# A one-core decoder step: all rotations on VectorE, fewer small VectorE steps, the normaliser in four strips

## The reference, cut to what matters

```python
xn = rms_norm(x, norm_w)
aq, ak, av, az, mq, mk, mv, mo, mz, ga, gm, mi, mf = split(xn @ w_in)
aq = partial_rope(rms_norm(aq, q_norm_w), pos)     # per head of 128
ak = partial_rope(rms_norm(ak, k_norm_w), pos)
# partial_rope: of 128 channels the first 32 are rotated, halves of 16
out = concat([x1 * cos - x2 * sin, x2 * cos + x1 * sin, rest])
attn = softmax(q k / sqrt(128)) v                  # prompt causal; samples over cached pages
# the samples take, of 4 blocks of 256 cached keys, the 3 with the best mean score
# matrix memory (mLSTM), state C, n, m:
h = num / maximum(abs(den), exp(-m_t))
den = w_inter * (q . n_prev) + sum(s)
n_new = a_prev * n_prev + sum_s a_s k_s
C_new = a_prev * C_prev + sum_s a_s k_s v_s^T
y = x + (sigmoid(ga) * (attn * silu(az)) @ Wa + sigmoid(gm) * (h * silu(mz)) @ Wm) @ w_out
```

## Time and profile before

| | us |
|---|---|
| median of three runs | 473.07 (472.76 to 473.12) |
| profiled execution | 472.86 |
| its span, first to last instruction | 470.7 |

### The profile page before, as it was taken

One profiled execution on the slowest core, in us unless ns is written; L12 is line 12 of the kernel. 1 busy time (PEld: TensorE's weight loads), 2 busy tenths in 40 slices (PEclk: granted clock), 3 DMA queues, 4 the chain that ended last, 5 costly groups with the idle time before them and its releaser, 6 DMA issues.

```text
span 470.7 us, 11313 instructions
## 1 busy us (share of the span) xinstructions
PE 458.8 (97%) x3823; PEld 417.4 (89%) x3823; DVE 402.6 (86%) x1646; ACT 289.5 (61%) x486; POOL 99.8 (21%) x181
## 2 busy tenths in 40 slices
PE   7999999999989999989999999999999999999997
PEld 5899899898779898878899889899899898899997
DVE  4898899699999997999999999889999874667861
ACT  4866545676973685995485695657848357324430
POOL 2040421013323322422321342312223110000000
PEclk9999999999999999999999999999999999999999
DMA  8899599659999999999999999998999995457511
GB/s 302 321 360 406 179 369 325 226 168 350 297 415 407 411 347 335 394 398 411 408 368 313 404 415 408 410 359 304 378 415 408 410 348 192 141 174 270 179 50 46
DMA packets 44993, 150.89 MB, mean 321 GB/s; under 512 B 6332, under 2 KB 7932, under 8 KB 44808
## 3 DMA queue, kind: packets, MB, share of 16 engines
q1 hardware_dynamic: 20368, 70.77, 41.3%
q0 software_dynamic: 19008, 67.20, 37.2%
q10 hardware_dynamic: 5560, 12.21, 6.7%
HBM read 137.37 MB, written 12.76 MB: 319 GB/s over the span
## 4 chain that ended last, share of the span: by engine, by line
PE 69%; DVE 15%; ACT 8%; issue 4%; DMA 3%; ACTq 0%; POOLq 0%; POOL 0%; DVEq 0%
PE pj L535 26%; PE pj L538 13%; PE wk L535 6%; DVE kpages L1169 4%; PE pa L716 4%; DVE wlo L1070 4%; PE wk L538 3%; DMA kpages<-in_cache_k 3%; DVE cslot L1253 2%; ACT L837 2%; ACT whi L817 2%; PE wk L488 2%; PE wk L640 2%; PE wk L672 1%; PE wk L493 1%
## 5 line engine op out<-in xcount | busy, mean ns | idle before, releaser
L535 PE MATMUL pj<-xn,whi 128*128 128x264 f32 x1328 | 180.6, 288 | 0.8 <-ACT mqT L975 0.7
L535 PEld LDWEIGHTS pj<-xn,whi 128*128 128x128 f32 x1328 | 168.4, 189 | 8.8 <-issue 6.6
L1070 DVE TENSOR_TENSOR wlo<-wraw,whi 128x1024 fp32r<-128x1024 f32 x112 | 137.1, 1228 | 8.7 <-ACT whi L817 8.2
L817 ACT ACTIVATE whi<-wraw 128x1024 fp32r<-128x1024 f32 x112 | 117.9, 1053 | 23.2 <-PE wk L538 13.0
L1169 DVE CUSTOM_DVE_ANT_0 kpages<-kpages,qbc 128x128 f32<-128x128 f32 x512 | 114.9, 288 | 1.7 <-DMA kpages<-in_cache_k 1.6
L538 PE MATMUL pj<-xn,wlo 128*128 128x264 f32 x664 | 94.3, 284 | 3.4 <-DVE wlo L1070 3.4
L538 PEld LDWEIGHTS pj<-xn,wlo 128*128 128x128 f32 x664 | 85.5, 188 | 4.5 <-DVE wlo L1070 4.5
L405 POOL DMA_DIRECT2D kpages<-in_cache_k x64 | 34.3, 536 | 175.2 <-DVE sco L1169 152.2
L405 POOL DMA_DIRECT2D vpages<-in_cache_v x64 | 33.9, 530 | 59.1 <-issue 40.1
L1169 DVE DVE_READ_ACCUMULATOR2_ANT sco<- 128x1 f32 x512 | 41.2, 80 | 0.0
L716 PE MATMUL pa<-vpages,prob 128*32 128x256 f32 x512 | 34.3, 385 | 0.7 <-ACT prob L875 0.7
(11 more groups left out here) (277 smaller groups left out, 634.7 us busy)
## 6 DMA issues: line engine op xcount, KB each, us to landing
wraw<-in_weights SPq DMA_DIRECT2D x112, 512.0 KB, 6.7
kpages<-in_cache_k POOLq DMA_DIRECT2D x64, 512.0 KB, 8.3
vpages<-in_cache_v POOLq DMA_DIRECT2D x64, 512.0 KB, 10.9
cslot<-in_states SPq DMA_DIRECT2D x16, 512.0 KB, 8.6
out_C_s<-cslot ACTq DMA_DIRECT2D x16, 512.0 KB, 8.0
xres<-in_tokens SPq DMA_DIRECT2D x1, 1056.0 KB, 6.8
out_k_p<-kT ACTq DMA_DIRECT2D x4, 256.0 KB, 9.8
out_v_p<-v_nat ACTq DMA_DIRECT2D x4, 256.0 KB, 5.0
```

The source lines that it names most:

```text
L535: mm(bank[:, 0:T], whi[:, q, k, :], src[:, g, k, :], start=(k == 0 and g == 0), stop=False)
L817: A(whi[:, n % WSPLIT], wraw[:, n % WRAW], ACT.Copy).then_inc(whi_ready, 1)
L1070: V.tensor_tensor(wlo[:, n % WRAW], wraw[:, n % WRAW], whi[:, n % WSPLIT], ALU.subtract).then_inc(wlo_ready, 1)
```

## The change

- The 32 rotated channels of a head are reordered in the weights, so that the two halves of 16 start 32 partitions apart (`ORDER`: 16 rotated, 16 others, 16 rotated, the rest). Then VectorE can make the rotation by itself: it multiplies partitions 32 to 63 by sin and writes to 0 to 31, and the other way round, and the signs are in the sine table. The product with `rot` is gone on TensorE, for queries and keys, and with it the waits for its bank; `rope_norm` has five instructions, four of which work on 32 or 64 partitions.
- The query rows are made by a product with the permutation `back` instead of by a transpose.
- The eight instructions on the rows of the gates all stand ahead of head 0.
- The new normaliser is made in four strips of 32 partitions: weights are a column of `wt` repeated 32 times, 64 columns of `mk_nat` move, eight products instead of four; the output's layout follows.
- On VectorE: `nm` comes out of the reductions (scale -SCALE, minimum), the `gmax` copy is gone, the two mask additions are one, the samples' denominator is made from already weighted products (order at step 6 changed, two instructions fewer at step 9).

```diff
-            def norm_sums(ss, ro, i, src):
-                mm(ss[:, 0:T], ones, sq[:, i, :], start=True, stop=True)
-                mm(ro[:, 0:T], rot, src, start=True, stop=True).then_inc(norm_ps, 1)
+            def norm_sums(ss, i):
+                mm(ss[:, 0:T], ones, sq[:, i, :], start=True, stop=True).then_inc(norm_ps, 1)
...
                     if g >= 2:
-                        pe.wait_ge(q_ready, g - 1)
+                        pe.wait_ge(rs_ready, g - 1)
...
-                    last = tr(bank[0:NB, (h - first) * P:(h - first + 1) * P], qT[:, h, SEQ:T], P)
+                    last = mm(bank[0:NB, (h - first) * P:(h - first + 1) * P], qT[:, h, SEQ:T], back, start=True, stop=True)
...
-                    for d in range(EC):
-                        for t in range(2):
-                            col = SEQ - 1 if t == 0 else 383
-                            last = mm(wk[3][:, MHD + d:MHD + d + 1], mk_nat[:, t, d * P:(d + 1) * P], wt[:, col:col + 1],
-                                      start=(t == 0), stop=(t == 1))
+                    part = MHD // VG
+                    for t in range(2):
+                        col = SEQ - 1 if t == 0 else 383
+                        for q in range(VG):
+                            last = mm(wk[3][q * VC:(q + 1) * VC, MHD:MHD + part], wt[:, col:col + 1].broadcast_to([P, VC]),
+                                      mk_nat[:, t, q * part:(q + 1) * part], start=(t == 0), stop=(t == 1))
...
+            def rope_norm(x, r, done):
+                low, high, both = slice(0, LO), slice(LO, 2 * LO), slice(0, 2 * LO)
+                ch.step(V.tensor_tensor(hT[low, 0, :], x[high], sin[high], ALU.mult))
+                ch.step(V.tensor_tensor(hT[high, 0, :], x[low], sin[low], ALU.mult))
+                ch.link(V.tensor_tensor(hT[both, 1, :], x[both], cos[both], ALU.mult))
+                ch.link(V.tensor_tensor(x[both], hT[both, 0, :], hT[both, 1, :], ALU.add))
                 V.tensor_tensor(x, x, r, ALU.mult).then_inc(done, 1)
...
-                if h == 1:
+                if h == 0:
                     dve.wait_ge(gate_ln, 1)
...
-                if h == 2:
...
-                if h == 3:
...
-                    ch.step(V.tensor_copy(gmax[:, b, :], gm[:, b % 2, :]))
                     V.tensor_tensor(probs[:, b % 2], sco[:, b % 2],
-                                    gm[:, b % 2, :].unsqueeze(1).broadcast_to([P, PAGES, HEADS]), ALU.subtract).then_inc(pm_ready, 1)
+                                    gmax[:, b, :].unsqueeze(1).broadcast_to([P, PAGES, HEADS]), ALU.subtract).then_inc(pm_ready, 1)
...
-                    V.tensor_scalar(nm[:, n, :], nm[:, n, :], -SCALE, None, ALU.mult).then_inc(smax_ready, 1)
+                    V.tensor_tensor_reduce(att[:, n, 0:P], wk[n][:, 0:P], mask3[:, 0:P], -SCALE, 3.0e38, ALU.add, ALU.min, nm[:, n, 0:1])
+                    V.tensor_tensor_reduce(att[:, n, P:384], wk[n][:, P:384], mask3[:, P:384], -SCALE, 3.0e38, ALU.add, ALU.min,
+                                           nm[:, n, 1:2]).then_inc(smax_ready, 1)
...
-                    ch.step(V.tensor_tensor(wt[:, 0:P], wt[:, 0:P], triT, ALU.add))
-                    V.tensor_tensor(wt[:, SEQ:384], wt[:, P:SEQ], triT, ALU.add).then_inc(wl_ready, 1)
+                    V.tensor_tensor(blocks, wt[:, 0:SEQ].rearrange("p (i t) -> p i t", i=2), triT.unsqueeze(1).broadcast_to([P, 2, P]),
+                                    ALU.add).then_inc(wl_ready, 1)
...
-                    ch.step(V.tensor_tensor(sst[:, 0], qk, w_new, ALU.mult))
-                    V.tensor_tensor(sst[:, 1], qn, w_old, ALU.mult).then_inc(qc_read, 1)
+                    ch.step(V.tensor_copy(sst[:, 0], qk))
+                    ch.link(V.tensor_tensor(sst[:, 2], qn, m_exp, ALU.max))
+                    V.scalar_tensor_tensor(out=sst[:, 2], in0=qn, scalar=-1.0, in1=sst[:, 2], op0=ALU.mult, op1=ALU.max).then_inc(qc_read, 1)
                     dve.wait_ge(qc_read, j + 1)
-                    ch.link(V.tensor_tensor(sst[:, 1], sst[:, 1], sst[:, 0], ALU.add))
-                    ch.link(V.tensor_tensor(sst[:, 2], sst[:, 1], m_exp, ALU.max))
-                    ch.link(V.scalar_tensor_tensor(out=sst[:, 2], in0=sst[:, 1], scalar=-1.0, in1=sst[:, 2], op0=ALU.mult, op1=ALU.max))
```

## The result

The changed kernel takes 478.12 us (median of 4 runs, 477.62 to 480.47) against 473.1 for the kernel before: a ratio of 1.0115 with a 95% interval of 1.0091 to 1.0138. It is slower by 5.0 us by the medians and 5.4 us by the ratio, outside the range of the prediction, on the side to which I gave 24%. The profiled execution took 477.62 us, with a span of 475.5 and a mean granted clock of 0.993.

What follows compares the result with a forecast made beforehand. TensorE and VectorE take turns as the bound. Terms +0.4 - 0.88 + 0.1 + 0.2 + 0.1 + 0.2 + 0.1 - 0.13 - 0.4 sum to -0.3 us: execution 472.5, median 472.8; range 470.0 to 475.1.

Steps and rivals of the forecast that it cites:

- TensorE's head period: Heads, before 50 us: removing the rotation saves TensorE 0.44 us a head, 3.1 us over seven; project 8 ends at 45.0.
- VectorE's rotation: Heads: five steps instead of four, 2.09 us instead of 1.74, +0.35 a rotation (bounds 0 to +0.46), +2.8 over eight heads.
- Rival D: VectorE suffers more: slower products from SBUF, or rotation chained at 0.46 throughout, +0.2 a rotation in 16: 474.4 us; 12%.
- Gates' rows: Moved ahead of head 0 into VectorE's 1.9 us idle time; transfer moves under 1 us, 5 us of slack, no cost or gain.
- Query rows: Behind the wait for the last head: eight products with `back` replace transposes, +0.88 us; step 1's project starts +0.4 later.
- Rival A: The late clock: the wait at 45 to 48 us drops TensorE to the lower level, +2.3 us, 475.1 in all; 16%.
- Round 0: Up to 93.6 us, TensorE leads: two key rotations removed, -0.88 us, and the normaliser's strips +0.1.
- 93.6 to 137: VectorE leads: one longer rotation, +0.35 us, less a `gmax` copy and a mask start-up of about 0.08 each: +0.2.
- 181 to 212: Taken as a copy of the VectorE-led stretch from 93.6 to 137.4 us: +0.2 us.
- 137 to 181 and 212 to 254: Later stretches of the rounds, TensorE leading from 137: +0.1 us each.
- Round 3: Close handover at `wlo`: VectorE +0.2 later against 0.33 spare, so only about 0.13 of TensorE's 0.88 us is gained: -0.13.
- From 306.7: VectorE leads: two instructions of the samples' normaliser removed, one replaced by a copy (0.26 us), and two `gmax` copies (0.15): -0.4.

Runs made afterwards that it cites:

- e4_forms: Changed kernel with the two sine products of query heads 1 to 5 replaced by forms on other partitions, rotation not computed there; ran once, 476.76 us.
- e3_rotation: Kernel before with all rotations on VectorE and query rows by products with `back`, gates' rows left where they were; 481.84 us, ratio 1.0195.
- e13: Changed kernel with the query rows' group behind chunk 9 instead of 8 and five products without use ahead of it; 477.73 us, ratio 1.009.
- e14: Changed kernel with query rows' group behind chunk 9, five products without use ahead, and gates' rows sent ahead of the seven V pages; 475.9 us, ratio 1.0052.
- e1_warm: Changed kernel with nine products without use on TensorE ahead of its wait for the last head; 477.3 us, ratio 1.0096.
- e6b_queries_te: Changed kernel with query rotations back on TensorE, keys on VectorE, the rotation's matrix with 128 columns; 476.08 us, ratio 1.0053.
- e7_behind: Changed kernel with the query rows' group behind chunk 9 instead of chunk 8; 475.66 us, ratio 1.0051.
- e6_queries_te: Changed kernel with query rotations back on TensorE, keys on VectorE, the rotation's matrix with 64 columns; 477.74 us, ratio 1.0105.

## Why the prediction was wrong, step by step

- *What bounds the kernel.* Right: TensorE leads in the head stage and VectorE from 93.6 on. "Work added on VectorE costs only where VectorE leads" was applied with the old leaders. The change itself makes VectorE the leader of the head stage, as my own sum said, and I didn't price what follows from a wait of that length.
- *TensorE's head period* 3.81 to 3.37: step 0 begins 3.1 us earlier. Right.
- *VectorE's rotation.* The first failed step: 0.35 us for the fifth instruction, taken from the spacing of an unchained one. The rotation got 0.55 us longer, and it starts 0.11 later behind a split, 0.66 in all, by three changes of blocks (e4_forms). That is 0.20 more than I had in each of eight heads and 0.11 in the six with a split in front, 2.3 us; the last head came at 50.20 instead of 48.1, 2.1 later. My upper bound, +0.46, didn't take this in, because I bounded the added instruction and not its neighbours. Rival D had the direction and the spacing (0.46 throughout, though by changes of blocks and not by waits) and, with 0.2 a rotation, two thirds of the size.
- *Gates' rows.* Right that they fill VectorE's idle time: without it 1.7 us more (e3_rotation). Right that their transfer is issued hardly earlier (34.3 instead of 35.0). That it lands later, at 50.7 instead of 48.4, and becomes the next bound once the clock is mended, I had not seen (e13, e14). The 5 us of slack were too many: in e13 it lands 6.0 us later than before and step 9 is 2.86 late, so some 3 us were to spare.
- *Query rows* +0.88: right (2.11 against 1.23 us at the full clock).
- *The clock.* The second failed step: the sum has nothing for it. Rival A, at 16%, is what happened. I held the 1.8 us before L504 as evidence against it and put its price at 2.3 us; it cost 1.75. Its weight was the real mistake: a wait of 3 us had no example in the trace of before, so nothing there spoke against the loss. Behind TensorE's idle 5.2 us the granted clock is 0.50, as that rule has it (the Trainium skill, TensorE: Matmul & The Clock Gate, "Part 1: The HAM clock gate"). Forecast +0.4 at step 1, measured +4.25 = 1.62 + 0.88 + 1.75.
- *Round 0*: forecast -0.78, measured from +4.35 at step 1's low half to +3.14 behind the strips, -1.21. The two rotations gave 0.90; the strips gave 0.31 instead of costing 0.1. I took the passes of 256 columns as the nearest row, with passes of 0.03 us as the bound (16 of them are 0.48 us, a gain of 0.31 and not of 0.35 as I wrote); the measured pass is 0.36 / 16 = 0.023 us.
- *93.6 to 137*: forecast +0.2, measured +3.12 to +3.67, +0.55, the key rotation's real 0.66. *181 to 212*: +0.2, measured +0.56. *137 to 181 and 212 to 254*: +0.1 each, measured +0.12 and +0.16, by luck: the forecast was dearer strips alone, and measured are waits behind the key rotation (+3.67 to +4.13, +4.35 to +4.83) less cheaper strips (0.34 and 0.32).
- *Round 3*: forecast -0.13, measured +0.96 from 236 to 311. The handover was close, 0.33 us of spare; two rotations of 0.66 each go past it, +1.53 up to 302, and 0.57 come back over the stretch of the strips. Of what TensorE saves there, 0.44 us go into a longer wait for ScalarE's `prob` (1.62 us at 282.05 instead of 0.74), an engine that my sum for this stretch left out.
- *From 306.7*: forecast -0.4, measured -0.70. It falls at one place (+5.67 at 374.36, +4.97 at 378.20), where TensorE waited 0.42 us for VectorE's page scores before and doesn't any more; that the removed instructions alone do this is not shown.
- *The sum*: +4.35 - 1.21 + 0.55 + 0.12 + 0.56 + 0.16 + 0.96 - 0.70 = +4.8, against -0.3. Of the 5.1 us between them 3.95 are lost by step 1's low half (+4.35 against +0.4).

## What to carry to other kernels

When work is moved to the engine that was behind, work out who leads the stage afterwards, and price the wait that comes of it twice if TensorE is the one that waits. Of a new instruction ask what its neighbours pay as well as what it takes. And follow a result that is made earlier to its transfer's place in the queue: until that place moves, nothing has moved.

## What the runs showed of the hardware that I had not expected

- On VectorE an f32 product of 264 columns starts 0.34 to 0.35 us after the one in front if both work from the same block of 32 partitions on, 0.44 to 0.46 if the block changes; behind a split it is 1.15 against 1.26 us (e4_forms).
- Waits of 2.05 to 2.33 us of TensorE were followed by a granted clock at the 1.2 GHz level in e1_warm (139.64), e4_forms (139.48), e6b_queries_te (137.75), e7_behind (50.32 and 138.25), e13_behind_warm (140.66) and e14_rows_early (137.43), and not in the profiles of the changed kernel (141.12, wait 2.07), e6_queries_te (139.96, wait 2.05) and e3_rotation (143.98, wait 2.04). From 137.45 to 145.45 of the table the first lose 1.55 to 1.59 us and the others 0.35, so the low clock costs some 1.2 us there; in e7_behind the query rows took 3.56 us instead of 2.11. The same kernel does it in one run and not in another: in e14_rows_early the runs with a mean clock of 1.0 took 474.5 and 475.42 us, those at 0.996 476.38 and 476.46.
- A weight matrix of 64 columns between two of 128 made the stretch around it 0.44 us longer, though it has less to load (e6_queries_te); over a whole head it was 0.34.
- The same 8 KB transfer, issued at 34.3 to 35.0 us on GpSimd's queue behind the same eleven loads, landed after 13.4 us (before), 16.0 (e7_behind), 16.4 (the changed kernel), 18.0 (e1_warm) and 20.0 (e13_behind_warm). The cause stays open: a faster head stage of TensorE, which frees weight buffers and so brings more loads beside it, could be behind the first step, but e7_behind and e13_behind_warm run alike up to 47.9 us and still differ by 4 us.
